# Matmuls of a three-product projection ordered by token half instead of alternating between halves

## The reference, cut to what matters

```python
x = x + mixer(rmsnorm(x))
x = x + jnp.square(jax.nn.relu(rmsnorm(x) @ W1)) @ W2     # W1 (1024, 4096), W2 (4096, 1024)
```

## Time and profile before

| | us |
|---|---|
| median of 3 runs (lowest, highest) | 1550.57 (1548.83, 1551.72) |
| the profiled execution: its time | 1550.17 |
| the profiled execution: span from first to last instruction | 1548.2 |
| TensorE matmuls busy | 1444.2 (93% of the span) |
| VectorE busy | 728.3 (47%) |
| ScalarE busy | 497.2 (32%) |
| mean granted TensorE clock | 0.948 of full speed |

### The profile page before, as it was taken

How to read it: one execution, slowest core, us unless ns; L and a number is a source line. 1 busy time by engine, 2 the same in 40 slices (tenths; PEclk the granted TensorE clock), 3 DMA queues, 4 the chain that set the end, 5 groups by cost and what they waited for, 6 DMA issues and landing times.

```text
span 1548.2 us, 33865 instructions
## 1 busy us (share of the span) xinstructions
PE 1444.2 (93%) x15054; PEld 1384.7 (89%) x15054; DVE 728.3 (47%) x906; ACT 497.2 (32%) x617; POOL 0.2 (0%) x4
## 2 busy tenths in 40 slices
PE   5899998898889689999999999999589999999998
PEld 4899997878879677599999999999479999999998
DVE  7745257575763332644433334333684333343332
ACT  5433234343423315232313123132143222131233
POOL 0000000000000000000000000000000000000000
PEclk7999999999999758899999999999799999999999
DMA  5123200000000404022222222321222223222221
GB/s 150 55 82 109 89 2 3 4 3 4 2 3 3 62 19 109 28 82 83 82 88 90 93 81 81 97 90 56 67 69 83 83 81 108 81 81 83 85 76 58
DMA packets 108888, 100.92 MB, mean 65 GB/s; under 512 B 21552, under 2 KB 106872, under 8 KB 108786
## 3 DMA queue, kind: packets, MB, share of 16 engines
q1 hardware_dynamic: 108786, 99.36, 21.0%
HBM read 94.18 MB, written 5.18 MB: 64 GB/s over the span
## 4 chain that ended last, share of the span: by engine, by line
PE 86%; DVE 8%; issue 3%; DMA 1%; SPq 1%; ACT 1%; ACTq 0%; DVEq 0%
PE ps L541 64%; PE ps L594 6%; PE ps L555 2%; PE ps L569 1%; PE ps L766 1%; DVE pool_sum L1989 1%; PE ps L678 1%; PE ps L775 1%; PE ps L607 1%; PE ps L718 1%; PE ps L871 1%; PE ps L904 1%; PE ps L1015 1%; PE ps L1014 1%; DVE wkv_OT L1647 1%
## 5 line engine op out<-in xcount | busy, mean ns | idle before, releaser
L541 PE MATMUL ps<-xs_hi,w_hi 128*128 128x272 f32 (+1 forms) x2656 | 556.3, 291 | 16.5 <-DVE xs_lo L1879 8.6
L541 PE MATMUL ps<-xs_hi,w_lo 128*128 128x272 f32 (+1 forms) x2656 | 554.3, 291 | 0.0
L541 PE MATMUL ps<-xs_lo,w_hi 128*128 128x272 f32 (+1 forms) x2656 | 552.3, 290 | 0.0
L541 PEld LDWEIGHTS ps<-xs_hi,w_hi 128*128 128x128 f32 (+1 forms) x2656 | 420.3, 189 | 20.5 <-issue 11.1
L541 PEld LDWEIGHTS ps<-xs_lo,w_hi 128*128 128x128 f32 (+1 forms) x2656 | 420.3, 190 | 0.5
L541 PEld LDWEIGHTS ps<-xs_hi,w_lo 128*128 128x128 f32 (+1 forms) x2656 | 417.4, 190 | 0.5
L1445 DVE TENSOR_TENSOR w_lo<-w_raw,w_hi 128x2048 fp32r<-128x2048 f32 (+1 forms) x83 | 188.6, 2273 | 165.1 <-ACT w_hi L1116 164.4
L1116 ACT ACTIVATE w_hi<-w_raw 128x2048 fp32r<-128x2048 f32 (+1 forms) x83 | 157.0, 1891 | 291.6 <-PE ps L541 286.1
L1797 DVE TENSOR_TENSOR x_res<-x_res,ps 128x544 f32<-128x544 f32 x64 | 46.1, 720 | 207.4 <-PE ps L541 207.4
L1260 ACT ACTIVATE square_tmp<-relu_tmp 128x544 f32<-128x544 f32 x64 | 42.1, 659 | 268.1 <-DVE relu_tmp L1791 268.1
L1791 DVE SCALAR_TENSOR_TENSOR relu_tmp<-ps,rstd 128x544 f32<-128x544 f32 x64 | 46.3, 723 | 129.8 <-PE ps L541 129.5
(11 more groups left out here) (311 smaller groups left out, 1397.9 us busy)
## 6 DMA issues: line engine op xcount, KB each, us to landing
w_raw<-in_ffn_w SPq DMA_DIRECT2D x64, 1024.0 KB, 5.2
w_raw<-in_rwkv_w_rkv SPq DMA_DIRECT2D x12, 1024.0 KB, 5.5
w_raw<-in_rwkv_w_o SPq DMA_DIRECT2D x4, 1024.0 KB, 5.1
x_rows<-in_x_prompt SPq DMA_DIRECT2D x4, 512.0 KB, 5.1
smp_state_rows<-in_state_wkv SPq DMA_DIRECT2D x8, 256.0 KB, 6.7
out_wkv_sample<-smp_state_out SPq DMA_DIRECT2D x8, 256.0 KB
out_y_prompt<-y_rows SPq DMA_DIRECT2D x4, 512.0 KB
w_raw<-in_rwkv_g SPq DMA_DIRECT2D x2, 640.0 KB, 5.3
```

Source lines behind the costliest of these rows:

```text
L541: mm = nc.tensor.matmul(bank(j, h)[0:w, 0:TH], wt[:, kw, c0:c0 + w], xt[:, kx, h * TH:(h + 1) * TH], start=(begins and n == 0 and wt is wh ...
```

## The change

Inside `pe_unit` the loop over the two token halves moves from the innermost place to the outermost place within a job. A job still issues the same 48 matmuls with the same operands into the same two banks. First come the 24 matmuls of half 0, over all k, and then the 24 of half 1. The wait `ready` for tile k is issued in the pass of half 0 alone. The signal `filled` still comes with the last matmul of the job.

```diff
                 ks = ktiles[m] if ktiles else [(k, k) for k in range(KT)]
-                for n, (kw, kx) in enumerate(ks):
-                    if ready is not None:
-                        ready(pe, m, kx)
-                    for wt, xt in ((wh, xh), (wh, xl), (wl, xh)):
-                        for h in range(2):
+                for h in range(2):
+                    for n, (kw, kx) in enumerate(ks):
+                        if ready is not None and h == 0:
+                            ready(pe, m, kx)
+                        for wt, xt in ((wh, xh), (wh, xl), (wl, xh)):
                             mm = nc.tensor.matmul(bank(j, h)[0:w, 0:TH], wt[:, kw, c0:c0 + w],
                                                   xt[:, kx, h * TH:(h + 1) * TH],
                                                   start=(begins and n == 0 and wt is wh and xt is xh),
```

## The result

The changed kernel takes 1570.02 us (median of 4 runs, 1567.92 to 1571.57), and the kernel before takes 1551.14 (1548.83 to 1554.34, 4 runs). The ratio is 1.0119, with a 95% interval from 1.0097 to 1.0142: slower by 1.2%. The forecast was 1565, with a range from 1558.5 to 1571. The profiled execution took 1571.57 us, with a span of 1569.6, which is 21.4 us more than the profiled execution of before.

What follows compares the result with a forecast made beforehand. TensorE was taken to bound the kernel; delays of 9.8 us (down units), 2.6 (first low-rank unit) and 2.3 (first W_o unit) sum to 14.7 on the profiled 1550.17, giving 1565 us, range 1558.5 to 1571.

Steps and rivals of the forecast that it cites:

- TensorE sets the time, so a delay stays: Whole kernel: TensorE holds 86% of the chain, so a delay there before the end delays the end.
- Down units, 1.23 us each: Eight feed-forward down units: hidden tiles 6 and 7 are now needed before their low parts land; 9.8 us in all.
- the rival of the falling clock: Down units: the clock drops to half speed at each new stall, 24 us on top, 1589; chance 6%.
- First low-rank unit, 2.6 us, and what follows it, between -1.3 and +0.4: 21 more matmuls after the last tile: 2.6 us, up to 4.8; clock at the second start -1.3 to +0.4, counted as nothing.
- First unit of W_o, 2.3 us: TensorE waits for nearly every tile; 18 more matmuls follow the last ones: 2.3 us at full rate, 4.1 at low.
- Sum of the waits, 14.7 us: Down, first low-rank and first W_o units together: 9.8 + 2.6 + 2.3 = 14.7 us.
- The rate, costed at nothing: Line 541's 7,968 matmuls: staying in a bank costs the same as switching, judged from fp32 mean rows; zero.
- The rival of a slower rate: Line 541: adding to the bank still being written waits, or loads stop hiding; 0.01 us per matmul, 80 us, 1645; chance 3%.
- the stay in a bank: Line 541: neighbours keep one bank for 24 matmuls; a rival had this faster, up to 96 us, 1469, chance 5%.
- Every matmul loads its weights already, so nothing is lost there: Line 541: 2,656 loads for 2,656 matmuls of a product, so losing shared weights between neighbours costs zero.
- the early delays are made good: Low-rank and W_o units: something other than TensorE sets the path to 710 us, their 4.9 us vanish, 1560; chance 6%.
- the waits do not come: Down units: waiting products are fetched some other way than in written order, only 4.9 us remain, 1555; chance 3%.

## Why the prediction was right, and where it was not

- *TensorE sets the time, so a delay stays.* Right. All delays are still there at the end of the table, and putting back the down units alone gave some 10 us back (9.6 in the traces). The first down unit starts 9.3 us later (757.64 to 766.91) where about 5 was said: 3.1 of that are the start and the scan, about 1 is the rate.
- *Down units, 1.23 us each.* Measured 1.17, with the two waits in the places that were worked out (0.60 us of idle time at tile 6, a short one at tile 7). Its parts were off and made each other good: the first matmul after a wait costs 0.10 us more, not 0.20, so tile 7 is waited for 0.15 us instead of 0.05, and 0.05 is the rate. The clock stayed at full speed over all eight, so the rival of the falling clock is out.
- *First low-rank unit, 2.6 us, and what follows it, between -1.3 and +0.4.* The unit lost 4.3 us up to its end (13.42 to 17.74), since the clock rose later against the last tile; about 0.6 us came back in the next unit, whose matmuls no longer fell to the low clock, and 0.9 behind the second start. Together 2.74 us, inside the bounds. The clock's part was taken at its low end, and the part behind it at zero; the two errors cancelled, which is luck. Most of the 0.9 is no effect of the change: from the second start to r it is 13.4 to 14.6 us in the traces with the late waits and 13.3 to 14.6 in those with the early ones.
- *First unit of W_o, 2.3 us.* Measured 2.49.
- *Sum of the waits, 14.7 us.* Measured 14.6. The early waits in the old order gave 15.7 without any of the new order.
- *The rate, costed at nothing.* This step failed, by 0.55 ns per matmul, some 4 us in all. That is most of the way from 1565 to 1570; the waits came out as forecast. That 1570 still lies in the range is luck in this respect: the upper end left room for a low clock behind the last tiles, not for the rate. The rival of a slower rate, given 3% and 80 us, came true in kind at a twentieth of its price. The rows that were taken for it are rounded to 0.01 us, and over 7,968 matmuls that is 80 us; they can't show what was asked of them. They are also of another kind, fp32 with two records per matmul. And the cause named for a change of the rate, the stay in a bank, was the wrong one: with the banks of either order exchanged, the rate stayed with the order of the operands. Both kernels have the same loads and the same matmuls, so a spacing set by the two together does not tell the orders apart.
- *Every matmul loads its weights already, so nothing is lost there.* The trace agrees: the changed kernel has the same 2,656 loads for each product. That rule of the Trainium skill ("TensorE: Matmul & The Clock Gate", section "Step-by-step: what each phase is for") had nothing to act on here. The figure of 3,984 that the prediction worked out for it is wrong: within a tile of the old order four matmuls in a row use `w_hi` and two use `w_lo`, so one load for each run would be 2,656 in all, and 5,312 in the new order. The term of zero does not hang on it.

The rivals in which the early delays are made good, or the waits do not come, are excluded by the same rows.

## What to carry to other kernels

Before a loop is reordered, ask for each operand after how many instructions it is needed and how many are left behind it once it is there. Moving an inner loop out halves the first number and raises the second, and an operand made by a chain that begins with the work just done has little slack to give (1.5 us here, where the change asks 2.3 to 2.6 us earlier). The other direction pays: where the engine waits for tiles as they arrive, put all work that a tile allows next to the tile, so that little is left behind the last one (6.5 us of 1551 at one place here, in part because TensorE, no longer idle, was at its full clock). And a term of "nothing" on 8,000 instructions needs rows that resolve a nanosecond: take two starts far apart and divide.

## What the runs showed of the hardware

The rate of such a stream takes a few fixed values. Waitless units ran at 0.12500, 0.12528, 0.12583 or 0.12611 us per matmul, each within 0.00002 in nearly every unit of a trace. The last two belong to orders in which neighbouring matmuls read the same half of the activations; in runs of 24 only the pass of half 0 is slower, 0.1264 against 0.1253. The first two both occur in the alternating order, and within one execution it can change from one to the other between units. What sets them was not found. The first matmul after a wait is 0.1 us longer to the next one at full speed (0.23 instead of 0.125 us, at 769.94), where the prediction took 0.2 from the start of the up projection.
